# First attention with scores as keys by queries, maxima of a rounded product, sums on GpSimd and no turns of the exponentials

## The reference

```
sc = jnp.einsum('bhgqd,bhkd->bhgqk', qi, kh, preferred_element_type=F32)
p = jax.nn.softmax(sc, axis=-1).astype(vh.dtype)
return jnp.einsum('bhgqk,bhkd->bhgqd', p, vh)
...
x = x + jnp.concatenate([y_pool, y_mlstm, y_attn], axis=-1) @ w_out[layer]
x = x + mem_cross_attn(rmsnorm(x, norm_mem_g[layer]), mem, ca_wq[layer], ca_wkv[layer], ca_wo[layer])
x = x + ec_moe(rmsnorm(x, norm_ffn_g[layer]), router_w[layer], expert_w_gu[layer], expert_w_down[layer])
```

## Time and profile before

| | |
|---|---|
| median of 3 runs | 1777.38 us (1776.68 to 1779.5) |
| the profiled execution | 1778.6 us |
| its span | 1776.9 us |
| TensorE busy | 1662.0 us, 94% |
| VectorE busy | 599.3 us, 34% |
| ScalarE busy | 461.1 us, 26% |
| GpSimd busy | 239.6 us, 13% |
| HBM read and written | 486 MB, 427 GB/s from about 400 to 1280 us |

### The profile page before, as it was taken

The page is one execution under the profiler, slowest core; times in us unless marked ns, Lnnn a source line. Parts: engine busy times, 40 slices in busy tenths (PEclk is TensorE's granted clock), DMA queues, the critical chain, the costliest instruction groups (busy, mean ns, idle before and its releaser), DMA issues.

```text
span 1776.9 us, 21438 instructions
## 1 busy us (share of the span) xinstructions
PE 1662.0 (94%) x8805; PEld 966.8 (54%) x8805; DVE 599.3 (34%) x1076; ACT 461.1 (26%) x889; POOL 239.6 (13%) x115
## 2 busy tenths in 40 slices
PE   8999999999999989989889798899999999999998
PEld 6897686743434324333233243333385558978886
DVE  5996784531200202002002020010086451350074
ACT  6457626300000000000000000000175433353242
POOL 0005412000000000000000000000030674116330
PEclk9999999999999999999999999999999999999999
DMA  9434056389999999999999999999930005212121
GB/s 346 140 132 131 1 166 252 145 355 427 427 428 427 429 428 428 429 428 429 429 428 429 428 428 429 427 419 428 415 110 17 32 13 118 96 41 103 56 99 48
DMA packets 69461, 486.06 MB, mean 274 GB/s; under 512 B 10540, under 2 KB 20229, under 8 KB 42639
## 3 DMA queue, kind: packets, MB, share of 16 engines
q1 hardware_dynamic: 69391, 485.06, 67.7%
HBM read 482.64 MB, written 2.41 MB: 273 GB/s over the span
## 4 chain that ended last, share of the span: by engine, by line
PE 72%; DMA 19%; DVE 5%; ACT 2%; issue 2%; POOL 0%; POOLq 0%; ACTq 0%; SPq 0%; DVEq 0%
PE psum L602 21%; PE psum L2161 14%; DMA ring<-in_expert_w_gu 12%; PE psum L2252 10%; DMA ring<-in_expert_w_down 6%; PE psum L2144 3%; PE psum L2266 3%; PE psum L3336 2%; PE psum L765 2%; PE psum L3012 2%; PE psum L743 2%; PE psum L730 2%; PE psum L3027 1%; PE psum L1838 1%; PE psum L2977 1%
## 5 line engine op out<-in xcount | busy, mean ns | idle before, releaser
L2161 PE MATMUL psum<-ring,work_area 128*64 128x512 f32 x2048 | 455.0, 596 | 52.5 <-DMA ring<-in_expert_w_gu 52.3
L2161 PEld LDWEIGHTS psum<-ring,work_area 128*64 128x64 f32 x2048 | 142.6, 137 | 345.9 <-issue 251.4
L2252 PE MATMUL psum<-ring,work_area 128*64 128x512 f32 x1008 | 227.6, 600 | 6.5 <-DMA ring<-in_expert_w_down 4.6
L2372 DVE TENSOR_TENSOR work_area<-psum,work_area 128x512 f32<-128x512 f32 x32 | 20.6, 686 | 592.8 <-ACT work_area L2310 592.8
L2310 ACT ACTIVATE work_area<-psum 128x512 f32<-128x512 f32 x32 | 17.4, 594 | 522.3 <-PE psum L2161 522.3
L2252 PEld LDWEIGHTS psum<-ring,work_area 128*64 128x64 f32 x1008 | 73.0, 137 | 133.7 <-issue 118.9
L2574 POOL TENSOR_TENSOR hn<-x_res,extra 128x1024 f32<-128x1024 f32 x2 | 4.7, 2368 | 861.8 <-DVE x_res L2386 861.8
L2454 POOL TENSOR_TENSOR block_lo<-ring,part_hi 128x1024 fp32r<-128x1024 f32 x35 | 85.6, 2455 | 159.3 <-ACT part_hi L2447 158.9
L602 PE MATMUL psum<-h_hi,part_hi 128*128 128x512 f32 x240 | 93.9, 391 | 1.0 <-DVE hn L886 1.0
L602 PE MATMUL psum<-h_hi,block_lo 128*128 128x512 f32 x240 | 93.4, 389 | 0.0
L602 PE MATMUL psum<-h_lo,part_hi 128*128 128x512 f32 x240 | 93.4, 389 | 0.0
(11 more groups left out here) (556 smaller groups left out, 2754.8 us busy)
## 6 DMA issues: line engine op xcount, KB each, us to landing
ring<-in_expert_w_gu SPq DMA_DIRECT2D x123, 2048.0 KB, 31.6
ring<-in_expert_w_down SPq DMA_DIRECT2D x58, 2048.0 KB, 28.4
ring<-in_w_in SPq DMA_DIRECT2D x12, 2048.0 KB, 8.6
ring<-in_expert_w_gu SPq DMA_DIRECT2D x10, 1024.0 KB, 8.8
ring<-in_expert_w_down SPq DMA_DIRECT2D x8, 1024.0 KB, 7.7
extra<-in_w_mod SPq DMA_DIRECT2D x4, 1536.0 KB, 9.3
ring<-in_w_out SPq DMA_DIRECT2D x3, 2048.0 KB, 14.1
hn<-in_w_mod SPq DMA_DIRECT2D x2, 1536.0 KB, 7.1
```

The costliest lines, as they stand in the source:

```text
L2161: ins = pe.matmul(psum[h * 64:(h + 1) * 64, c, :], xsT[:, k, e * CAP:(e + 1) * CAP], w[:, (2 * c + h) * BANK:(2 * c + h + 1) * BANK], star ...
L2252: ins = pe.matmul(psum[n * 64:(n + 1) * 64, 6, :], hidT[b][:, j, h, :], w[:, j, n * BANK:(n + 1) * BANK], start=(q == 0 and j == 0), stop= ...
```

## The change

The first attention takes the second one's form. A tile is 128 keys by 512 queries of two heads: four pairs of heads, four tiles each, 16 tiles. `fa_rough_pe` multiplies the rounded queries and keys alone, two heads side by side over 1024 columns; `fa_max_dve` reduces them to negated maxima; `fa_turn_pe` turns four of those, `fa_rows_act` copies the two rows, and `fa_exact_pe` adds them to the tile's three products as a fourth one with one row of ones. Rounded products 0 to 3 stand ahead of everything, in four pairs of banks; 4 and 5 follow tile 0, 6 and 7 tile 1, and then one follows each tile, all in banks 4 and 5. The exponential needs neither bias nor accumulated sums. GpSimd adds the four exponentials of a pair of heads (`fa_sums_pool`), `fa_sums_pe` sums them over the partitions, and `fa_divide_dve` takes one reciprocal of 512 columns for each pair and multiplies `ymixT` with it; the first of the four stands between the reductions 12 and 13, the others behind reduction 15. In GpSimd's queue `mlstm_scale_pool` is split off `mlstm_norm_pool`, and the order is now written out in the program's list.

```diff
--- before.py
+++ after.py
@@ -333,8 +333,11 @@
         ca_wo = cut(slot(3), 0, CA_H, D)
         rope_t = [slot(6)[:, i * 1024:(i + 1) * 1024] for i in range(2)]
         max_rows = cut(x_flat, 0, 2, ML_H, S)
-        p_at = [slot(6)[:, 2048 + i * S:2048 + (i + 1) * S] for i in range(4)]
-        pt_at = [cut(slot(7), i * 2048, T, S) for i in range(2)]
+        fa_p = [cut(slot(7), i * 2 * S, 2, S) for i in range(4)]
+        fa_total = [cut(slot(6), 2048 + i * 2 * S, 2, S) for i in range(2)]
+        fa_row = [rounded(f"fa_row{i}", 7168 + i * S, S, base=W_at) for i in range(2)]
+        fa_ones, fa_recip = rounded("fa_ones", 3072, P, base=x_at), x_flat[:, 3200:3200 + S]
+        fa_max = [cut(const, C_COS, T, 64), cut(x_flat, 3712, T, 64)]
         hn_ca = cut(ring, four, T, D)
@@ -1057,7 +1060,7 @@
         def round_ymix(k):
 
             B.full(act, g_qT[-1])
-            B.drained(act, g_pool[k] if k < 2 else g_mlT[k - 2] if k < 4 else g_attn[2 * (k - 4) + 1])
+            B.drained(act, g_pool[k] if k < 2 else g_mlT[k - 2] if k < 4 else g_fa_sums[k - 4])
@@ -1535,11 +1538,11 @@
             pool.wait_ge(sem("small_in"), 16 * 5)
             for g in g_o:
                 B.drained(pool, g)
+            pool_link(pool.tensor_tensor(sig_o, sig_o, ml_g.unsqueeze(1).to_broadcast([P, T, ML_H * HD]), ALU.mult))
+        def mlstm_scale_pool():
             flat = hsum.rearrange("p t h d -> p t (h d)")
-            pool_link(pool.tensor_tensor(sig_o, sig_o, ml_g.unsqueeze(1).to_broadcast([P, T, ML_H * HD]), ALU.mult))
-
-            rest_of_ymix(0, 1)
-            rest_of_w_out(4, 8)
             pool.wait_ge(sem("recip_ready"), 1)
             rs = stat[:, 16:32].rearrange("p (t h) -> p t h", t=T).unsqueeze(3).to_broadcast([P, T, ML_H, HD])
             pool_link(pool.tensor_tensor(hsum, hsum, rs, ALU.mult))
@@ -1661,19 +1664,200 @@
...
-        attn_pe, attn_act, attn_dve, g_attn_end = attention(
-            [(i, i + 4) for i in range(4)], S,
-            lambda h, qt: score_part(0, S, *three_products((qT_hi[half(h), h % 4, qt * P:(qt + 1) * P], qT_lo[half(h), qt, h % 4, :]),
-                                                           (kT_hi[half(h), :], kT_lo[half(h), :]))),
-            values_at(lambda h, kt: av[:, kt, half(h)], T, 2 * P), HD, p_at, pt_at,
-            scaled_out(lambda i, q: by_rows(ymixT[:, 4 + i, :], q.start // GRID_W, q.stop // GRID_W), False), step=2,
-            besides={(dve, 22): mlstm_mean_dve, (act, 23): mlstm_root_act, (dve, 24): mlstm_recip_dve,
-                     (act, 5): lambda: round_ymix(0), (act, 6): lambda: round_ymix(1),
-                     (act, 8): lambda: round_w_out(4, 5), (act, 10): lambda: round_w_out(5, 6),
-                     (act, 12): lambda: round_w_out(6, 7), (act, 14): lambda: round_w_out(7, 8),
-                     (act, 18): lambda: round_ymix(4), (act, 26): lambda: round_ymix(5)}, outs=g_attn)
+        FA_PAIRS, FA_TILES = AT_H // 2, AT_H // 2 * T
...
+        fa_roughs_at = [(4, 5), (6, 7)] + [(i + 6,) if i + 6 < FA_TILES else () for i in range(2, FA_TILES)]
+        fa_order = [("rough", n) for n in range(T)]
+        for i in range(FA_TILES):
+            fa_order += [("exact", i)] + [("rough", n) for n in fa_roughs_at[i]]
+        fa_scored_at = {what: fa_scored + n + 1 for n, what in enumerate(fa_order)}
...
+        g_fa_out = [B.take_at(6) for c in range(FA_PAIRS)]
+        g_fa_sums = [B.take_at(7) for c in range(FA_PAIRS)]
+        g_attn_end = g_fa_sums[-1]
...
+        def fa_summed_at(i):
+            c, kt = i // T, i % T
+            return 4 + c * (T - 1) + max(kt, 1) + (1 if c >= 2 else 0)
+        def fa_rough_bank(n):
+            return (4, 0, 2, 6)[n] if n < T else 4
+        def fa_rough_pe(n):
+            c, qt = n // T, n % T
+            if n >= T:
+                pe.wait_ge(fa_maxed_sem, fa_maxed + n)
+            for j in range(2):
+                ins = pe.matmul(psum[:, fa_rough_bank(n) + j, :], qT_hi[at_head(j), c, qt * P:(qt + 1) * P], kT_hi[at_head(j), :],
+                                start=True, stop=True)
+            ins.then_inc(fa_scored_sem, 1)
+        def fa_turn_pe(c):
+            pe.wait_ge(fa_maxed_sem, fa_maxed + (c + 1) * T)
+            if c >= 3:
+                B.drained(pe, g_fa_sums[c - 3])
+            for qt in range(T):
+                ins = pe.transpose(psum[0:33, 7, qt * P:(qt + 1) * P], fa_max[c % 2][:, qt, 0:33], ident)
+            ins.then_inc(fa_turned_sem, 1)
+        def fa_exact_pe(i):
+            c, kt = i // T, i % T
+            keys = slice(kt * P, (kt + 1) * P)
+            if i < 2:
+                pe.wait_ge(fa_maxed_sem, fa_maxed + i + 2)
+            else:
+                pe.wait_ge(fa_exped_sem, fa_exped + i - 1)
+            for n, (k, q) in enumerate(((kT_hi, qT_hi), (kT_lo, qT_hi), (kT_hi, qT_lo))):
+                for j in range(2):
+                    r, to = at_head(j), psum[:, 2 * (i % 2) + j, :]
+                    if q is qT_lo:
+                        pe.matmul(to.rearrange("p (t q) -> p t q", t=T), k[r, keys], q[r, :, c, :], start=False, stop=False)
+                    else:
+                        pe.matmul(to, k[r, keys], q[r, c, :], start=(n == 0), stop=False)
+            if i == 0:
+                fa_turn_pe(0)
+            if kt == 0:
+                pe.wait_ge(fa_taken_sem, fa_rows_taken + c + 1)
+            for j in range(2):
+                ins = pe.matmul(psum[:, 2 * (i % 2) + j, :], fa_ones[one_row(j), :], fa_row[c % 2][one_row(j), :],
+                                start=False, stop=True)
+            ins.then_inc(fa_scored_sem, 1)
+        def fa_values_pe(i):
+            c, kt = i // T, i % T
+            g = g_fa_out[c]
+            if kt == 0:
+                B.acquire(pe, g)
+            pe.wait_ge(fa_exped_sem, fa_exped + i + 1)
+            for j in range(2):
+                ins = pe.matmul(B.at(g)[at_head(j), :], av[:, kt, at_head(j)], fa_p[i % 4][:, j, :],
+                                start=(kt == 0), stop=(kt == T - 1), skip_group_check=True)
+            if kt == T - 1:
+                B.filled(ins, g)
+        def fa_sums_pe(c):
+            g = g_fa_sums[c]
+            pe.wait_ge(sem("pool_step"), fa_summed_at(c * T + T - 1))
+            pe.wait_ge(fa_taken_sem, fa_rows_taken + min(c + 3, FA_PAIRS))
+            B.acquire(pe, g)
+            for j in range(2):
+                ins = pe.matmul(B.at(g)[at_head(j), :], ones[:, 0:HD], fa_total[c % 2][:, j, :],
+                                start=True, stop=True, skip_group_check=True)
+            B.filled(ins, g)
+        def attn_pe():
+            for g in fa_before:
+                B.drained(pe, g)
+            for n in range(T):
+                fa_rough_pe(n)
+            for i in range(FA_TILES):
+                c, kt = i // T, i % T
+                fa_exact_pe(i)
+                if kt == 2 and c + 1 < FA_PAIRS:
+                    fa_turn_pe(c + 1)
+                for n in fa_roughs_at[i]:
+                    fa_rough_pe(n)
+                if i >= 1:
+                    fa_values_pe(i - 1)
+                if kt == 2 and c >= 1:
+                    fa_sums_pe(c - 1)
+            fa_values_pe(FA_TILES - 1)
+            fa_sums_pe(FA_PAIRS - 1)
+        def fa_rows_act(c):
+            act.wait_ge(fa_turned_sem, fa_turned + c + 1)
+            for j in range(2):
+                ins = act.activation(fa_row[c % 2][one_row(j), :], psum[32 * j:32 * j + 1, 7, :], ACT.Identity)
+            ins.then_inc(fa_taken_sem, 1)
+        def fa_out_act(c):
+            g = g_fa_out[c]
+            B.full(act, g)
+            B.release(copy(act, by_rows(ymixT[:, 4 + c, :]), rows_of(B.at(g))), g)
+        def attn_act():
+            act.activation(fa_ones[:], ones, ACT.Identity)
+            fa_rows_act(0)
+            behind = {1: lambda: round_ymix(0), 3: lambda: round_ymix(1), 4: lambda: round_w_out(4, 5), 6: mlstm_root_act,
+                      7: lambda: round_w_out(5, 6), 8: lambda: round_w_out(6, 7), 9: lambda: round_w_out(7, 8),
+                      11: lambda: round_ymix(4), 15: lambda: round_ymix(5)}
+            for i in range(FA_TILES):
+                c, kt = i // T, i % T
+                act.wait_ge(fa_scored_sem, fa_scored_at["exact", i])
+                if i >= 4:
+                    act.wait_ge(sem("pool_step"), fa_summed_at(i - 4))
+                first = 2 * (i % 2)
+                act.activation(fa_p[i % 4], psum[:, first:first + 2, :], ACT.Exp).then_inc(fa_exped_sem, 1)
+                if kt == 2 and c + 1 < FA_PAIRS:
+                    fa_rows_act(c + 1)
+                if kt == 0 and c >= 1:
+                    fa_out_act(c - 1)
+                if i in behind:
+                    behind[i]()
+            fa_out_act(FA_PAIRS - 1)
+        def fa_max_dve(n):
+            c, qt = n // T, n % T
+            first = fa_rough_bank(n)
+            dve.wait_ge(fa_scored_sem, fa_scored_at["rough", n])
```

(36 more changed lines are left out.)

15 lines of the change are left out of this document (13 added, 2 removed).

## The result

| | before | after |
|---|---|---|
| median | 1778.44 us (4 runs, 1776.68 to 1780.77) | 1806.68 us (4 runs, 1804.39 to 1809.31) |
| the profiled execution | 1778.6 | 1806.94 |
| its span | 1776.9 | 1805.2 |
| granted clock, mean | 0.997 | 0.988 |

The ratio is 1.0158, 95% interval 1.0139 to 1.0178: 28.2 us slower where 16.1 was forecast. It lies outside the range (1784 to 1802). Measured a second time, the ratio was 1.0144 (1.0127 to 1.0160).

A forecast was written before the change was run, and what follows sets the result against it. The chain through TensorE's attention, then VectorE's modulation sums to the second norm's start, was taken as the bound. That start moves 14.6 us later, plus 1.5 for the clock: 16.1 on the median 1777.4 gives 1793.5 us, range 1784 to 1802.

The forecast's parts named there:

- the turns of the two engines: Behind the attention, line 1329's VectorE operations take 2.3 us or longer instead of 1.28, alternating with GpSimd's weight parts.
- the common shift of the later marks: All marks after the second norm's first addition shift by the same amount as it, 14.6 us before the clock term.
- the last sums: At the attention's end, they wait for GpSimd's addition (2.38 us) after the last exponential; 226.3, sign range 224 to 231.
- the second norm: Its first residual addition on VectorE comes at 271.7, 14.6 us later than before; sign range 267 to 277.
- the clock: TensorE's clock falls in the emptier attention start and at the stall; between nothing and twice 1.7 us, taken as 1.5.
- The third rival: Low clock and longer stalls: TensorE's 5 us before 183 take twice as long; 1799, up to 1803 us; chance 0.08.
- Plain work: TensorE in the attention: 2.14 us a tile, 0.25 a rounded pair; 44.8 us in all against 55.1, without waits.
- Start: Attention start waits for maxima of four query tiles: first exponential at 174.3, tile 2's scores at 180.9.
- Stall: The first division stands between VectorE's reductions 12 and 13; TensorE waits for reduction 13 and loses 4.6 us.
- Tail: VectorE after the last sums: reciprocal, multiply and copy from 226.4 to 232.3, 9.2 us later than 223.12 before.
- GpSimd beside the sums: GpSimd's remaining w_out low parts and six ymix_lo take turns with VectorE's modulation sums: 9.3 us of waiting.
- TensorE after this, no new bound: TensorE's output projection ends at 277.3, before VectorE's last addition asks at 283.0.

The follow-up runs named there:

- both waits filled: Changed kernel plus unread filler multiplies on TensorE in the attention's start and 16 behind tile 8's exact products; 1797.76 us (ratio 1.0090), again 1801.49 us (1.0127).
- the start filled: Changed kernel plus 28 unread filler multiplies on TensorE while the attention's start waits for the maxima; 1804.83 us (ratio 1.0134), again 1803.79 us (1.0137).
- pieces run: Changed kernel with the first pair's reciprocal cut into three pieces behind reductions 13 to 15, bank 7 released by each reciprocal; 1798.61 us, ratio 1.0113.
- the two kernels without low parts: Changed kernel with GpSimd's low-part subtractions behind the attention cut to 8 columns: 1799.0 us; the same with reciprocal pieces and start fillers: 1789.86 us.

## Why the prediction was wrong

Right were the direction, the mechanisms and their order. Of the signs it named, the first exponential, the gap behind tile 8, the turns of the two engines and the common shift of the later marks came; the last sums (237.5 for 224 to 231) and the second norm (283.2 for 267 to 277) did not. The size was off by 12 us, and the step that failed is **the clock**: "Between nothing and twice 1.7 I take 1.5." It measured 5.6 us up to the second norm, and 1.8 behind it. The one pair of rows it was taken from the earlier trace rows had one fall with a quarter of the clock lost; the new start had half of it lost for 20 us, and behind the stall it took 1.5 and 3.0 us more. The third rival had this ("if the 5 us of TensorE's work before 183 take twice as long") at 1799 to 1803, and got 0.08; the measured time lies beyond it too.

By steps, counted from the first multiply. I had the second norm at 271.7 - 165.8 = 105.9 without the clock. With both waits filled, so that TensorE is at full clock nearly throughout, it measured 111.4; with the clock 117.0. The durations of the filled run below are those of its second profile.
- *Plain work*: 2.34 a tile for 2.14, 0.42 a rounded pair for 0.25. In the second attention five pairs take 1.36 of a tile's 2.37 and I took one away at 0.23; but here the starts lie 0.34, 0.23, 0.32 and 0.43 apart (in the filled run, the last of them the row of ones), and the long steps are those at which the shape of the operands changes. That reading has no experiment of its own, and a step from 64 to 33 rows in the second attention (1394.85 to 1395.08) is 0.23 all the same, so only the durations are shown. 14 x 0.20 + 8 x 0.17 = 4.2 us missing: the second mis-sized term.
- *Start*: first exponential 174.81 for 174.3, right; tile 2's scores 18.4 us behind the first multiply for 15.1, and 17.2 and 16.1 with the start filled. Of the last, 1.1 is the fillers' own, so the missing 3.3 are nearly all the clock.
- *Stall*: 3.17 us in the changed run for 4.6, 3.85 in the filled one, of which 0.5 is the fillers' own. The cause is right, the size 1.3 too large (ScalarE's root, a reciprocal of 3.29 for 3.4, a multiply of 2.25). An estimate by the Trainium skill's figure is 0.66 for that reciprocal (VectorE: DVE Perf Modes, The TRN2 errata); the trace has 3.29, and 3.36 for the later three.
- *Last sums*: I had them wait for GpSimd's addition, 2.5 us from the last values to their end. They wait for bank 7 instead, which the third multiply releases (2.80), and the clock falls in that wait: 4.8 us, 2.3 missing. The pieces run shows it: there bank 7 is released by the reciprocal, and what ends their wait is GpSimd's addition.
- *Tail*: 6.5 us for 6.0. In the changed kernel 7.1, the last multiply taking 2.82.
- *GpSimd beside the sums*: 37.2 us from sums to norm for 39.4; about 2 less, since another of the low parts had come to lie beside the last division. "They take turns, whole instructions at a time" was right.
- *TensorE after this, no new bound*: right, the output projection ended at 286.0, the last addition asked at 294.5.

Together 1.0 (the start, filled) + 4.2 - 0.8 + 2.3 + 0.5 - 2.2 = 5.0 of the 5.5; the waits of 0.24 and 0.66 us ahead of two of the sums are the rest, to within 0.4. The clock adds 5.6 - 1.5 = 4.1. By my estimate 1.6 of the 5.5 are the fillers' own and belong to the clock; the total is the same.

Behind the norm, from its last addition to the first expert product, it takes 105.0 us in the kernel before and 107.0 and 106.6 in the two profiles of the changed one, a place I had not looked at. This too is the clock. In all 16 profiles the query projection of the cross attention starts 7.9 us behind that addition. Its multiplies, of which these are the third in the changed kernel and the fourth in the second profile with both waits filled,

```profile
303.38 0.63 PE L1948 MATMUL psum<-hq_hi,ca_wq_hi 128*128 128x512 f32 x1
...
297.46 0.39 PE L1962 MATMUL psum<-hq_hi,ca_wq_lo 128*128 128x512 f32 x1
```

stand 0.43 us apart where the clock is still low (0.50 in 300 to 305 in the first of these), and 0.23 apart where it has come back (0.50 in 290 to 295 in the second, 0.88 in 295 to 300). Nine steps are wide in the first profile of the changed kernel and seven in the second, none in the kernel before: 1.8 us in the mean of the two times. 16.1 + 5.5 + 4.1 + 1.8 = 27.5, against the 28.2 and 25.6 measured.

## What to carry to other kernels

When a change makes TensorE wait for a few microseconds in the middle of dense work, price the work behind the wait at half the clock as well: here the work behind a wait of 3.2 us took 1.5 to 4.2 us longer than behind the same wait filled. A row of a wait elsewhere is no upper bound for it. And read such a cost by stretches: filled one after the other, two waits show shares that depend on the order.
Follow every instruction that a queue now does later to the engine that shares its memory then: moving four GpSimd subtractions by 40 us, with nothing else changed, cost 7.8 us. And a tail of two engines in turn gives back little of what is won ahead of it: 4.1 us sooner became 2.1.

## What the runs showed of the hardware

- TensorE's clock fell to 0.50 behind a wait of 3.15 us and stayed at 1.00 where the same wait was filled with multiplies whose results nobody reads. Fillers cost what they overrun: here 1.1 us at the start and 0.5 at the stall.
- At 1.2 GHz four value multiplies take 1.97 us for 1.08, a pair of scores 0.63 for 0.40.
- A reciprocal from PSUM takes 0.95 us for 128 columns, 1.75 for 256 and 3.29 to 3.36 for 512: some 6.3 ns a column; cut into 128, 128 and 256 columns it takes 3.65 in all.
- A multiply of 512 columns with both inputs in SBUF, one of them in a permuted view (`by_rows`), takes 1.24 and 1.19 us while GpSimd is idle (the two kernels without low parts), and up to 2.82 beside GpSimd.
- Between the second norm's last addition and the experts, five of the 16 profiles take 105.0 to 105.2 us and eleven 106.6 to 107.9. In the five no multiply at the head of the query projection stands 0.43 from the next; in the eleven 7 to 14 do, some 0.2 us each. Which of the two a run gets isn't set by the kernel: with both waits filled it was once 106.9, once 105.1.
